# Expert 0's input rows picked by matrix products with a one-hot table, and the residual scaling spread over four experts

## What is computed

```python
x = layer_norm(ALPHA * x + m, ln1_g[l], ln1_b[l])        # x1 in the kernel
f = grouped_moe(x, w_router, b_router, w_e1[l], w_e3[l], w_e2[l])
x = layer_norm(ALPHA * x + f, ln2_g[l], ln2_b[l])
...
s = jax.nn.sigmoid((xt @ w_router).astype(jnp.float32))  # 16 scores per token
gates = ...                                              # two experts per token
for e in range(N_EXPERTS):
    h = jax.nn.silu(xt @ w_e1[e]) * (xt @ w_e3[e])
    y = y + gates[:, e:e + 1] * (h @ w_e2[e])
```

## Time and profile before

| | |
|---|---|
| median of three runs | 776.56 us (776.21 to 778.88) |
| time of the profiled execution | 777.23 us |
| its span in the trace | 775.4 us |
| PE, DVE, ACT, POOL busy | 744.9, 606.1, 429.6, 72.4 us |
| position products end, first `hidden` product of expert 0 starts | 455.03, 467.90 us |
| one expert in the steady part (from one `turn_xg` to the next) | 17.69 us |

### The profile page before, as it was taken

How to read it: one execution, slowest core, us unless ns; L and a number is a source line. 1 busy time by engine, 2 the same in 40 slices (tenths; PEclk the granted TensorE clock), 3 DMA queues, 4 the chain that set the end, 5 groups by cost and what they waited for, 6 DMA issues and landing times.

```text
span 775.4 us, 10750 instructions
## 1 busy us (share of the span) xinstructions
PE 744.9 (96%) x3580; PEld 614.0 (79%) x3580; DVE 606.1 (78%) x819; ACT 429.6 (55%) x577; POOL 72.4 (9%) x96
## 2 busy tenths in 40 slices
PE   3999999999999999999999979999999999999995
PEld 3888878888888878888888857888888888888873
DVE  5699977676578847443448887999999999999977
ACT  5522145657322236423331457888888888888851
POOL 5000000000000000000011121111111111110314
PEclk9999999999999999999999979999999999999998
DMA  9734657233333451423287587999999999999582
GB/s 299 235 96 99 206 154 208 59 105 100 110 117 109 129 168 57 131 87 105 85 321 296 174 310 247 354 385 387 387 382 389 388 397 371 396 383 382 159 171 112
DMA packets 137489, 175.53 MB, mean 226 GB/s; under 512 B 15418, under 2 KB 75558, under 8 KB 137430
## 3 DMA queue, kind: packets, MB, share of 16 engines
q1 hardware_dynamic: 128896, 154.95, 58.8%
q0 software_dynamic: 7616, 19.34, 8.2%
q10 hardware_dynamic: 934, 0.69, 0.3%
HBM read 164.06 MB, written 19.11 MB: 236 GB/s over the span
## 4 chain that ended last, share of the span: by engine, by line
PE 91%; DVE 4%; ACT 3%; DMA 1%; issue 1%; POOL 0%; SPq 0%; DVEq 0%; ACTq 0%
PE bank L1836 27%; PE bank L1838 27%; PE bank L1837 27%; PE bank L2133 2%; PE bank L1831 1%; PE bank L2054 1%; DMA x_in<-in_x_sample_dram 1%; PE bank L2148 1%; PE bank L2234 1%; PE bank L1872 1%; PE bank L2093 1%; ACT probs L770 1%; ACT w_hi L718 1%; PE bank L1884 0%; DVE w_lo L1051 0%
## 5 line engine op out<-in xcount | busy, mean ns | idle before, releaser
L1051 DVE TENSOR_TENSOR w_lo<-raw,w_hi 128x1024 fp32r<-128x1024 f32 x103 | 125.1, 1221 | 78.6 <-ACT w_hi L718 78.4
L718 ACT CAST w_hi<-raw 128x1024 fp32r<-128x1024 f32 x103 | 107.0, 1048 | 102.2 <-PE bank L1838 98.8
L1836 PE MATMUL bank<-xT_hi,w_hi 128*128 128x512 f32 x352 | 139.0, 395 | 2.9 <-DVE xT_lo L1089 1.8
L1838 PE MATMUL bank<-xT_hi,w_lo 128*128 128x512 f32 x352 | 137.7, 391 | 0.0
L1837 PE MATMUL bank<-xT_lo,w_hi 128*128 128x512 f32 x352 | 137.6, 391 | 0.0
L1836 PE MATMUL bank<-w_hi,xgT_hi 128*128 128x512 f32 x198 | 80.1, 405 | 1.0 <-issue 1.0
L1836 PEld LDWEIGHTS bank<-xT_hi,w_hi 128*128 128x128 f32 x352 | 66.5, 189 | 17.9 <-issue 3.5
L1838 PEld LDWEIGHTS bank<-xT_hi,w_lo 128*128 128x128 f32 x352 | 66.4, 189 | 14.0
L1838 PE MATMUL bank<-w_hi,xgT_lo 128*128 128x512 f32 x198 | 77.5, 392 | 0.0
L1837 PE MATMUL bank<-w_lo,xgT_hi 128*128 128x512 f32 x198 | 77.3, 390 | 0.0
L1837 PEld LDWEIGHTS bank<-xT_lo,w_hi 128*128 128x128 f32 x352 | 66.4, 189 | 13.3
(11 more groups left out here) (289 smaller groups left out, 1517.2 us busy)
## 6 DMA issues: line engine op xcount, KB each, us to landing
raw_more<-in_w_e_dram SPq DMA_DIRECT2D x48, 512.0 KB, 6.3
raw<-in_w_e_dram SPq DMA_DIRECT2D x48, 512.0 KB, 7.2
raw_late<-in_w_e_dram SPq DMA_DIRECT2D x48, 512.0 KB, 6.7
raw_rows<-in_w_e_dram SPq DMA_DIRECT2D x48, 512.0 KB, 7.5
raw<-in_w_in_dram SPq DMA_DIRECT2D x28, 512.0 KB, 6.6
raw<-in_w_gate_dram SPq DMA_DIRECT2D x24, 512.0 KB, 3.8
y_scratch<-zeros SPq DMA_DIRECT2D x8, 512.0 KB, 5.1
raw<-in_w_o_dram SPq DMA_DIRECT2D x8, 512.0 KB, 3.8
```

What stands on the lines that cost most here:

```text
L718: act.copy(hi_slot(j), raw_slot(j)).then_inc(hi_cast, 1)
L1051: dve.tensor_tensor(lo_slot(j), raw_slot(j), hi_slot(j).bitcast(F32), ALU.subtract).then_inc(lo_cast, 1)
L1836: pe.matmul(out, hi_l, hi_r, start=start, stop=False)
L1838: return pe.matmul(out, lo_l, hi_r, start=False, stop=stop)
```

## The change

Expert 0 no longer gets its rows through a list, a gather and transposes. DVE makes a one-hot table of tokens by slots for expert 0 alone, straight from `position` (`first_slots`, fp32, in the room of `y`), and PE multiplies it with x1, which still lies in SBUF: the product is the transposed rows at once (`take_first`, two halves of 16 products of 128x128x128, fp32). The place in the order:

- DVE: `position`, `first_slots`, `most` and `joint` come ahead of the sums that give the gates. The lists of groups 0 and 1 are made in one step instead of two.
- PE: three filler products instead of ten, and earlier; then `take_first(0)`, `joint_slots` of groups 1 and 0 together, `take_first(1)`.
- POOL: one gather less. The memset that clears `xg` no longer waits for the copies of x1; it comes right after the last `root`.
- ACT: the four scalings of x1 leave their place ahead of the first `split_xg` and are done one each in experts 0 to 3, behind the cast of k = 2. For this two turns of ACT's loop over experts are written out.

```diff
-LISTS = 3
+LISTS = 2
...
+    first_slots = y[:, 0, 0:TT * SLOTS].rearrange("p (t s) -> p t s", t=TT)
...
-        act.wait_ge(x1_stored, 16 * TT)
-        scale_residual()
+        def scale_residual(t):
+
+            act.activation(x1[:, t, :], x1[:, t, :], ACT.Copy, scale=ALPHA).then_inc(x1_scaled, 1)
...
+                if k == 2 and residual is not None:
+                    scale_residual(residual)
...
-        with act.Fori(0, 7) as i:
+        act.wait_ge(x1_stored, 16 * TT)
+        for n in range(TT):
+            expert(n, n % 2, U_MOE + 4 + 12 * n, residual=n)
+        with act.Fori(0, 5) as i:
...
-        dve.wait_ge(dve_step, step(3))
+        dve.wait_ge(*filled("position"))
+        dve.scalar_tensor_tensor(out=position[:], in0=bank("position")[:, 0:64].rearrange("p (t e) -> p t e", t=TT),
+                                 scalar=1.0, in1=chosen, op0=ALU.add, op1=ALU.mult).then_inc(routed, 1)
+        dve.wait_ge(routed, 1)
+        dve.scalar_tensor_tensor(out=first_slots, in0=position[:, :, 0:1].to_broadcast([P, TT, SLOTS]), scalar=0.0,
+                                 in1=iota_one[:].unsqueeze(1).to_broadcast([P, TT, SLOTS]), op0=ALU.subtract,
+                                 op1=ALU.is_equal).then_inc(first_chosen, 1)
+        dve.tensor_reduce(most[:], bank("position")[:, 64:80], AX.X, ALU.max).then_inc(frees("position"), 1)
+        dve.tensor_reduce(joint[:], position[:].rearrange("p t (g k) -> p t k g", k=4), AX.X, ALU.add).then_inc(
+            dve_step, 1)
+        dve.wait_ge(dve_step, step(4))
...
-        joint_lists(0, 0)
-        dve.tensor_reduce(most[:], bank("position")[:, 64:80], AX.X, ALU.max).then_inc(frees("position"), 1)
-        joint_lists(1, 1)
+        joint_lists(0, 1, 0)
...
-        pool.wait_ge(x1_stored, 16 * TT)
+        pool.wait_ge(unit_used, U_MOE)
         pool.memset(xg[:], 0.0).then_inc(pool_step, 1)
         pool.wait_ge(pool_step, 2 * TT + 2)
-        gather(0, 0, 0)
-        gather(1, 1, 1)
-        pool.wait_ge(*m_filled(M_XT + 1, 0))
+        pool.wait_ge(x1_stored, 16 * TT)
+        gather(1, 1, 0)
         gather(2, 0, 2)
...
+        def take_first(half):
+
+            pe.wait_ge(*m_empty(M_XT + half, 0))
+            for k in range(4):
+                c = 4 * half + k
+                for t in range(TT):
+                    o = pe.matmul(psum[M_XT + half][:, k * P:(k + 1) * P], x1[:, t, c * P:(c + 1) * P],
+                                  first_slots[:, t, :], start=t == 0, stop=t == TT - 1)
+            o.then_inc(psum_full[M_XT + half], 1)
...
-        pe.wait_ge(routed, 1)
-        joint_slots(0, 0)
-        joint_slots(1, 1)
-        keep_busy(10)
-        turn_xg(0, 0, 0)
+        keep_busy(3)
+        for t in range(TT):
+            pe.wait_ge(x1_ready[t], 1)
+        pe.wait_ge(first_chosen, 1)
+        take_first(0)
+        joint_slots(0, 1, 0)
+        take_first(1)
```

More of the change, by code:

```diff
@@ L404, in encoder_layer @@
     flag_ready = sem("flag_ready")
+    first_chosen = sem("first_chosen")
     onehot_ready = sem("onehot_ready")
@@ L915, in _ @@
         cast_hi(U_MOE + 3)
-        def scale_residual():
-            for t in range(TT):
-                act.activation(x1[:, t, :], x1[:, t, :], ACT.Copy, scale=ALPHA).then_inc(x1_scaled, 1)
-        act.wait_ge(x1_stored, 16 * TT)
-        scale_residual()
+        def scale_residual(t):
+            act.activation(x1[:, t, :], x1[:, t, :], ACT.Copy, scale=ALPHA).then_inc(x1_scaled, 1)
         def split_xg(n, q):
@@ L946, in scale_y, with expert @@
                            scale=slot_gate[:, q:q + 1]).then_inc(psum_free[M_Y + half], 1)
-        def expert(n, q, j, per=0, i=None):
+        def expert(n, q, j, per=0, i=None, residual=None):
             for k in range(12):
@@ L966, in _ @@
         silu(U_MOE + 3, 0)
-        with act.Fori(0, 7) as i:
+        act.wait_ge(x1_stored, 16 * TT)
+        for n in range(TT):
+            expert(n, n % 2, U_MOE + 4 + 12 * n, residual=n)
+        with act.Fori(0, 5) as i:
             for q in range(2):
-                expert(i * 2 + q, q, U_MOE + 4 + 12 * q, 24, i)
+                expert(i * 2 + (TT + q), q, U_MOE + 4 + 12 * q, 24, i + 2)
         def copy_turned(s):
@@ L1033, in _ @@
                 act.wait_ge(x1_reloaded, 16 * TT)
-                scale_residual()
+                for t in range(TT):
+                    scale_residual(t)
                 scale_last(1)
@@ L1445, in _ @@
         sel = sel.bitcast(F32)
+        chosen = sel.rearrange("p t g e -> p t (g e)")
         dve.wait_ge(*drained("r_s"))
@@ L1464, in _ @@
         dve.tensor_copy(info[..., 2], gates[:]).then_inc(dve_step, 1)
[L1465 to L1468, removed]
         dve.wait_ge(dve_step, step())
         dve.tensor_tensor(info[..., 3], gates[:], info[..., 2].bitcast(F32), ALU.subtract).then_inc(dve_step, 1)
[L1471 to L1474, removed]
+        dve.wait_ge(dve_step, step())
         def make_onehot(e, q, b=0):
@@ L1563, in _ @@
             cast_lo(u)
-        joint_lists(2, 2, 3)
+        joint_lists(1, 2, 3)
         def expert(n, q, j, scatters, per=0, i=None):
@@ L1664, in _ @@
                         scatters = e * 3 + (EXPERTS // 2 - 1 + b)
-                        dve.wait_ge(gathered[0], (e * 3 + (EXPERTS // 2 + b)) * 16)
+                        dve.wait_ge(gathered[0], (e * 3 + (EXPERTS // 2 - 1 + b)) * 16)
                         dve.wait_ge(y_stored[0], scatters * 16)
@@ L2105, in joint_slots @@
         def joint_slots(n, *ks):
-            pe.wait_ge(onehot_ready, ks[-1] + 1)
+            pe.wait_ge(onehot_ready, max(ks) + 1)
             pe.wait_ge(*m_empty(M_INFO, n))
@@ L2157, in output @@
             tokens(j, k % 2, k % 2 == 1, [psum[M_Y + k // 2][:]], hT_hi, hT_lo, lambda x, t: x, per, i)
-        pe.wait_ge(routed, 1)
-        joint_slots(0, 0)
-        joint_slots(1, 1)
-        keep_busy(10)
-        turn_xg(0, 0, 0)
+        keep_busy(3)
+        for t in range(TT):
+            pe.wait_ge(x1_ready[t], 1)
[3 more added lines that the diff above has]
+        take_first(1)
         for k in range(4):
             hidden(M_H1, 0, 0, U_MOE + k, k)
-        joint_slots(2, 2, 3)
+        joint_slots(1, 2, 3)
         def expert(n, q, j, gathers, per=0, i=None):
@@ L2182, in _ @@
             for q in range(2):
-                expert(i * 2 + q, q, U_MOE + 4 + 12 * q, i + q, 24, i)
+                expert(i * 2 + q, q, U_MOE + 4 + 12 * q, i, 24, i)
         for n in (12, 13):
-            expert(n, n % 2, U_MOE + 4 + 12 * n, (n + 1) // 2)
+            expert(n, n % 2, U_MOE + 4 + 12 * n, n // 2)
         def turn_onehot(s):
@@ L2250, in _ @@
                         slots(e, e * 3 + (6 + b), e * 3 + (LISTS + b))
-                        turn_xg(n, 0, e * 3 + (EXPERTS // 2 + b))
+                        turn_xg(n, 0, e * 3 + (EXPERTS // 2 - 1 + b))
                         for k in range(4):
```

1 line of the change is left out of this document (removed).

## The result

Before and after were run side by side, 22 times each. The kernel before took 776.23 us (775.25 to 778.88), the changed one **778.31 us** (776.29 to 780.01). The ratio is **1.0023, with a 95% interval of 1.0015 to 1.0031**, that is 1.8 us longer. It was measured twice more on other chips: 1.0016 [1.0001, 1.0031] and 1.0014 [1.0001, 1.0028]. So the change costs 1.1 to 1.8 us by these ratios; the plain medians lie 2.1, 1.0 and 0.9 us apart. That is less than the 0.5% named in the prediction, and more than nothing.

A forecast was written before the change was run, and what follows sets the result against it. PE, busy 96% of the span, was taken as the bound, with DVE's queue holding expert 0's start. Terms -0.4, +0.7 and +1.2 us gave +1.5 us, so 778.1 us against the median 776.56; range 775.5 to 780.0 us.

The forecast's parts named there:

- the three terms: Parts of the forecast sum: -0.4 us for expert 0's earlier start, +0.7 for ACT's delays, +1.2 for TensorE's clock.
- DVE's queue binds the new start: Ahead of expert 0: DVE's unchanged casts, one-hot tables and split hold the first hidden product, so it starts only 0.4 us earlier.
- gains what it removes: Rival ahead of expert 0: 6.8 us of old chain removed, at most 2.9 us gained, 773.7; chance of 1.5 us or more 0.05.
- `take_first` half: 3.92 us: PE ahead of expert 0: sixteen fp32 products are 32 instructions of 0.1225 us each, 3.92 us at full clock.
- The idle time ahead of the first product: 2.5 us: PE between the end of take_first(1) at about 465.0 and hidden at 467.5: nothing to do for 2.5 us.
- ACT's scaling costs 0.7 us: Experts 0 to 3: moved scalings delay DVE's cast and h; PE waits 0.1 to 0.2 us in each, 0.7 in all.
- The memset holds nothing in its new place: POOL's memset beside DVE's normalising of x1: costed at nothing; the rival that it holds DVE 1.81 us had chance 0.04.
- The clock: +1.2 us at the likeliest: Near expert 0's first products: TensorE's clock falls after 2.5 us idle, costing about 1.2 us, upper bound 2.6.
- 0.52 against 0.32: Chance of the forecast with a clock fall near the first products, against the rival that the clock holds, 776.9 us.
- The sign that it named: Profile after the change: PEclk under 1.00 somewhere in 465 to 472 would show the clock's fall.
- Fillers ahead of `take_first`: Three fillers in the gap speak against the rival of a low clock already in take_first, 781.2 us, chance 0.07.
- the shorter copy: DVE's copy into r_kth after the position products: 1.15 us, read as held by the memset, expected under 0.3 us.

The follow-up runs named there:

- the reordered one: Changed kernel with the scaling behind k = 4 and the first half of DVE's split of expert 0's rows ahead of its casts: 774.23 us, ratio 0.9958.
- filled version: Changed kernel with ten filler products between take_first(1) and expert 0's first product: 777.15 us, ratio 1.0004; on another chip 777.73 us, 1.0001.

## Why the prediction held

The time was inside its range and 0.2 us from the forecast, and each of the three terms has the right sign. That it came so close is partly luck: the terms were off by -0.2, +0.3 and up to -0.3 us, which offset each other, and the kernel before came out at 776.23 us where 776.56 was reckoned with. By its steps:

- **DVE's queue binds the new start.** Right. It forecast a gain of 0.4 us (0.3 by its own rows, since 462.1 + 4.70 is 466.8 and not 466.7); the profile shows 0.58. The casts, the tables and the split follow each other without a gap, and taking them out of the way gives 3.0 us. The rival "gains what it removes" put at most 2.9 us there for an empty queue; the reordered one reached 12.87 - 9.28 = 3.6, as the products were faster than forecast. So the limit was well placed.
- **`take_first` half: 3.92 us.** It took 3.81 with its tail and 3.67 in the chain, 0.115 us an instruction instead of 0.1225. `first_slots` took 0.69 us, as forecast (0.68).
- **The idle time ahead of the first product: 2.5 us.** It was 2.77, because PE was done sooner and waited for the same queue.
- **ACT's scaling costs 0.7 us.** The mechanism is right to the row: DVE's second cast waits 0.67 us (forecast 0.73), `turn_h` waits in experts 0 to 3 and not in 4. The size was low: 0.245 us an expert, 0.98 in all. Its rows gave less than 0.1 us an expert (`h` done at 483.55, wanted at 483.47), and the hand-over of 0.15 us from `h` to PE was left out; the 0.7 was taken above them.
- **The memset holds nothing in its new place.** Right: two-input instructions of 128x1024 beside it took 1.22 us, as in the kernel before. The Trainium skill, GPSIMD Engine Reference, section 1 (Specifications), speaks of contention for such a pair; for a memset the traces here don't show it.
- **The clock: +1.2 us at the likeliest.** One fall costs 1.6 us, more than the 1.2 taken, but it doesn't come in every execution. Filling the idle time gave 1.0 to 1.2 us by the ratios and 0.9 by the count of falls, so as a mean the term was about right; as the price of one fall it was mis-sized. It was treated as a case that happens or doesn't (0.52 against 0.32), and both happened, in different executions of one kernel. The sign that it named, PEclk under 1.00 in 465 to 472, is in none of the three traces of the changed kernel.
- **Fillers ahead of `take_first`.** They were given the credit for a steady clock there. Without them one execution shows a fall at that place, and low clocks are somewhat more frequent, but the median doesn't tell; this stays open.

The sum, with the measured terms: -0.6 + 1.0 + 0.9 = +1.3 us, inside the measured 1.1 to 1.8. The forecast was +1.5. It used the shorter copy, but didn't see how much hangs on it: the moved memset alone makes the start 1.24 us earlier, and `take_first` in this order of DVE's work loses 0.66 us of that.

## What to carry to other kernels

When a path is replaced by a faster one, look at what else must be ready for the same consumer. Here the rows came sooner and the consumer waited as long, for a queue on another engine, and only after reordering that queue did the change pay, 4 us better than without. Look also for small edits that ride along: in the profile the moved memset alone brought the start forward by more than the change it belonged to. And count an idle stretch of TensorE at more than its length: if nothing useful can be put in, products for nobody can be cheaper than standing still. To price such a stretch, compare many executions with it and with it filled; one profile can miss it.

## What the runs showed of the hardware

- **Whether the clock falls after an idle time differs from one execution to the next.** All kernels here have the same idle time of 1.6 to 1.8 us at about 16 to 18 us, and 6 of 14 traces show the clock at 0.50 behind it. Behind the 2.77 us it fell in one of five traces. In the old order PE stood idle for 2.4 to 3.2 us behind the position products, and it fell in all three traces. Behind 0.45 us (ahead of `take_first`) and 0.47 us (ahead of the first product, filled version) it fell in none, and 1.24 us came with a fall in their one trace.
- **A short copy was held beside a memset, most two-input instructions weren't.** The copy of 128x16 took 1.15 us while the memset of POOL ran and 0.17 us when it didn't, while instructions of 128x1024 with two inputs took 1.22 us either way. Its neighbours in the kernel before, under the same memset:

```profile
454.29 0.22 DVE L1447 TENSOR_TENSOR r_tmp<-r_s,r_sel 128x64 f32<-128x64 f32 x1
...
454.51 1.07 DVE L1450 TENSOR_TENSOR info<-token_one,r_sel 128x64 fp32r<-128x64 f32 x1
```

The two-input instruction ahead of the copy took 0.22 us, as without the memset; the one right behind it began while the copy stood and ended with it, at 455.58 (0.27 us without the memset). Why the copy is held was not tested.

- **An fp32 product of 128x128x128** took 0.23 us, as two instructions of 0.115 us: 16 take 3.67 us, about as long as 16 `hidden` products of four times the columns (0.23 us each).
